# Row maxima of the attention scores from half-depth matmuls, two heads at once on the two halves of the array's rows, with the first pair issued one step earlier

## What is computed

```python
def one_block(qblk):
    s = jnp.einsum("bqkgd,bskd->bkgqs", qblk.astype(jnp.float32), kf) * scale
    p = jax.nn.softmax(s, axis=-1)
    return jnp.einsum("bkgqs,bskd->bqkgd", p, vf)
```

## Time and profile before

| what | value |
|---|---|
| median of 3 executions | 2594.71 us |
| lowest, highest | 2590.71, 2596.11 us |
| the profiled execution | 2592.71 us |
| span from its first to its last instruction | 2590.9 us |
| TensorE busy in the span | 96% |
| VectorE, ScalarE, GpSimd busy | 65%, 46%, 43% |
| mean granted TensorE clock | 0.99 of full |
| steps of phase2 (key heads 0 to 3) | about 929 to 1670 us |

### The profile page before, as it was taken

How to read it: one execution, slowest core, us unless ns; L and a number is a source line. 1 busy time by engine, 2 the same in 40 slices (tenths; PEclk the granted TensorE clock), 3 DMA queues, 4 the chain that set the end, 5 groups by cost and what they waited for, 6 DMA issues and landing times. The chain is left out here.

```text
span 2590.9 us, 40706 instructions
## 1 busy us (share of the span) xinstructions
PE 2477.0 (96%) x14413; PEld 2243.1 (87%) x14413; DVE 1692.4 (65%) x2527; ACT 1194.2 (46%) x2187; POOL 1101.8 (43%) x936
## 2 busy tenths in 40 slices
PE   5999999999999899999999989999899999999998
PEld 2899999999999887778878867799899999988886
DVE  5047456556558458787787767626977777776775
ACT  5223323323324246766666667645544444443442
POOL 1123132222223353433343233733667777756554
PEclk9999999999999999999999999999999999999999
DMA  9611111111111110010020010242122222245654
GB/s 328 207 35 45 36 52 44 37 43 44 37 43 30 50 34 9 11 54 9 9 65 9 1 55 27 91 119 74 48 72 76 76 76 76 76 159 204 222 199 142
DMA packets 193130, 195.66 MB, mean 76 GB/s; under 512 B 23516, under 2 KB 155772, under 8 KB 193020
## 3 DMA queue, kind: packets, MB, share of 16 engines
q1 hardware_dynamic: 191804, 189.52, 23.0%
q10 hardware_dynamic: 1216, 4.72, 0.5%
HBM read 162.22 MB, written 31.99 MB: 75 GB/s over the span
## 5 line engine op out<-in xcount | busy, mean ns | idle before, releaser
L395 PE MATMUL proj_ps<-act_hi,w_hi 128*128 128x384 f32 x1152 | 406.6, 353 | 3.3 <-ACTq L748 3.3
L397 PE MATMUL proj_ps<-act_hi,w_lo 128*128 128x384 f32 x1152 | 387.1, 336 | 0.0
L396 PE MATMUL proj_ps<-act_lo,w_hi 128*128 128x384 f32 x1152 | 386.9, 336 | 0.0
L571 POOL CAST w_hi<-w_raw 128x1024 fp32r<-128x1024 f32 x48 | 79.2, 1650 | 563.9 <-PE proj_ps L397 523.9
L1960 DVE TENSOR_TENSOR probs_lo<-mix_ps,probs_hi 128x512 fp32r<-128x512 f32 x324 | 222.9, 689 | 138.8 <-ACT mix_ps L1758 135.1
L2921 DVE SCALAR_TENSOR_TENSOR conv<-up,conv_t,conv 128x127 f32<-128x127 f32 (+4 forms) x264 | 242.1, 945 | 59.1 <-ACT conv L2701 53.5
L1757 ACT ACTIVATE probs_hi<-mix_ps 128x512 fp32r<-128x512 f32 x324 | 193.5, 597 | 174.8 <-PE mix_ps L1546 173.5
L395 PEld LDWEIGHTS proj_ps<-act_hi,w_hi 128*128 128x128 f32 x1152 | 217.6, 189 | 11.3 <-issue 4.3
L396 PEld LDWEIGHTS proj_ps<-act_lo,w_hi 128*128 128x128 f32 x1152 | 217.5, 189 | 2.8
L397 PEld LDWEIGHTS proj_ps<-act_hi,w_lo 128*128 128x128 f32 x1152 | 217.0, 188 | 0.0
L2969 DVE TENSOR_TENSOR sums_hi<-gated_raw,sums_hi 128x384 fp32r<-128x384 f32 x66 | 145.1, 2201 | 81.8 <-ACT sums_hi L2778 81.7
(11 more groups left out here) (341 smaller groups left out, 6895.7 us busy)
## 6 DMA issues: line engine op xcount, KB each, us to landing
w_raw<-in_w_down SPq DMA_DIRECT2D x66, 512.0 KB, 3.3
w_raw<-in_w_in SPq DMA_DIRECT2D x64, 512.0 KB, 3.8
w_raw<-in_w_up SPq DMA_DIRECT2D x44, 512.0 KB, 4.3
ada_w<-in_ada_w SPq DMA_DIRECT2D x7, 2048.0 KB, 15.8
gated_raw<-gated_scratch SPq DMA_DIRECT2D x66, 192.0 KB, 3.5
q_k_dec<-in_ada_w SPq DMA_DIRECT2D x5, 2048.0 KB, 7.9
gated_scratch<-gated SPq DMA_DIRECT2D x22, 288.5 KB, 2.1
gated_scratch<-gated SPq DMA_DIRECT2D x22, 287.5 KB, 2.1
```

What stands on the lines that cost most here:

```text
L395: nc.tensor.matmul(out, w_hi, x_hi, start=(k == 0), stop=False)
L396: nc.tensor.matmul(out, w_hi, x_lo, start=False, stop=False)
L397: return nc.tensor.matmul(out, w_lo, x_hi, start=False, stop=last)
```

## The change

The maxima are made from the high parts of the queries alone, over 64 rows of the array. The staging order of the queries is changed so that after the transpose heads 0 and 1 have their high parts on partitions 0 to 63, and heads 2 and 3 on partitions 64 to 127. `max_pair(s, j)` takes the place of `max_piece`: it waits until both banks are free and issues one matmul for a head of 0 and 1 on the lower 64 rows into `B_S` and one for the head two further on the upper 64 rows into `B_X`. The ten pieces keep their sizes; `PIECES` is reordered so that pieces 2j and 2j + 1 are pair j. Pair 0 of step s + 2 is issued at i = 9 of step s, behind `weighted`; pairs 1 to 4 of step s + 1 at i = 0 (behind `weighted`), 2, 4 and 6. For this `q_part(s + 2)` moves to i = 8, and `q_out(s + 2)` to i = 9 ahead of `exps(s + 1, 1)`. VectorE reduces the two pieces of pair 0 behind `low(s + 1, 1)`, and the others around `low`. In `context_step` the five pairs are issued with two fill units behind each from pair 2 on (key heads 0 and 3) or from pair 0 on (1 and 2), and pair 0 of the step after next at its end.

```diff
--- before.py
+++ after.py
@@ -1016,7 +1016,9 @@
         PL = sb("probs_lo", [P, 4, 512], F32R)
         QT1 = sb("q_t_hilo", [P, 2, 512], F32R)
         QT2 = sb("q_t_max", [HEAD + 1, 2, 512], F32R)
-        QS1 = sb("q_stage", [P, GQ, P], F32R)
+        QS1 = sb("q_stage", [P, 10 * HEAD], F32R)
+        Q_HI = QS1[:, :].rearrange("p (a c d) -> p a c d", a=2, d=HEAD)[:, :, 0:3:2, :]
+        Q_LO = QS1[:, HEAD:7 * HEAD].rearrange("p (a c d) -> p a c d", a=2, d=HEAD)[:, :, 0:3:2, :]
         QS2 = sb("q_stage_max", [P, GQ, HEAD + 2], F32R)
         ATT = sb("attn_t", [P, 2, T])
         ZA = sb("za_gate", [P, 2, T])
@@ -1114,9 +1116,9 @@
 
         S_USES = [(("k", 0, g), B_S) for g in range(4)] + [(("c", 0), B_S)]
 
-        PIECES = [(0, 0), (0, 1), (1, 0), (1, 1), (0, 2), (2, 0), (2, 1), (3, 0), (3, 1), (2, 2)]
+        PIECES = [(0, 0), (2, 0), (0, 1), (2, 1), (1, 0), (3, 0), (1, 1), (3, 1), (0, 2), (2, 2)]
         NP = len(PIECES)
-        PIECES_AT = [(0, 1), (2,), (3, 4), (5,), (6, 7), (8,), (9,), (), (), ()]
+        PAIR_AT = {0: 1, 2: 2, 4: 3, 6: 4}
         for s in range(NSTEP):
             kv, n = step_of(s)
             if n == 0 and kv + 1 < NKV:
@@ -1309,10 +1311,10 @@
                     if s:
                         pool.wait_ge(x_done, X_AT["q", s - 1] + 1)
                     pool.wait_ge(rope_ok, s + 1)
-                    q = QKV[:, n, 0:4 * HEAD].rearrange("p (h d) -> p h d", d=HEAD)
-                    nc.gpsimd.tensor_copy(QS1[:, :, 0:HEAD], q).then_inc(qs1_ok, 1)
+                    q = QKV[:, n, 0:4 * HEAD].rearrange("p (a b d) -> p a b d", a=2, d=HEAD)
+                    nc.gpsimd.tensor_copy(Q_HI, q).then_inc(qs1_ok, 1)
                     pool.wait_ge(qs1_ok, 2 * s + 1)
-                    nc.gpsimd.tensor_tensor(QS1[:, :, HEAD:P], q, QS1[:, :, 0:HEAD].bitcast(F32), ALU.subtract).then_inc(qs1_ok, 1)
+                    nc.gpsimd.tensor_tensor(Q_LO, q, Q_HI.bitcast(F32), ALU.subtract).then_inc(qs1_ok, 1)
 
                 def stage_q2(s):
                     kv, n = step_of(s)
@@ -1497,7 +1499,7 @@
                     pe.wait_ge(qs1_ok, 2 * s + 2)
                     pe.wait_ge(x_out, X_AT["q", s])
                     for h in range(GQ):
-                        m = nc.tensor.transpose(X[:, h * P:(h + 1) * P], QS1[:, h, :].bitcast(F32), ident[:, :])
+                        m = nc.tensor.transpose(X[:, h * P:(h + 1) * P], QS1[:, h * P:(h + 1) * P].bitcast(F32), ident[:, :])
                     m.then_inc(x_done, 1)
 
                 def q_max_part(s):
@@ -1517,20 +1519,28 @@
                         m = nc.tensor.matmul(bank[:, h * P:(h + 1) * P], QT1[:, s % 2, h * P:(h + 1) * P], KH[:, 0:P], start=True, stop=True)
                     m.then_inc(s_done, 1)
 
-                def max_piece(s, p):
-                    if p == 0:
+                def max_pair(s, j):
+                    if j == 0:
                         pe.wait_ge(x_out, X_AT["q", s] + 1)
                         pe.wait_ge(kh_out, 4 * (s // NS) + 4)
-                    pe.wait_ge(s_out, S_FREE["p", s, p])
-                    h, part = PIECES[p]
-                    bank = ps[:, (B_S, B_X)[p % 2], :]
-                    q = lambda h: QT1[:, s % 2, h * P:(h + 1) * P]
+                    pe.wait_ge(s_out, S_FREE["p", s, 2 * j])
+                    pe.wait_ge(s_out, S_FREE["p", s, 2 * j + 1])
+                    h, part = PIECES[2 * j]
+                    low, high = ps[:, B_S, :], ps[:, B_X, :]
+                    q_low = lambda h: QT1[0:HEAD, s % 2, h * P:(h + 1) * P]
+                    q_high = lambda h: QT1[HEAD:P, s % 2, (h + 2) * P:(h + 3) * P]
                     if part == 2:
+                        past = slice(9 * P, 11 * P)
                         for i in range(2):
-                            m = nc.tensor.matmul(bank[:, i * 2 * P:(i + 1) * 2 * P], q(h + i), KH[:, 9 * P:11 * P], start=True, stop=True)
+                            cols = slice(i * 2 * P, (i + 1) * 2 * P)
+                            m_low = nc.tensor.matmul(low[:, cols], q_low(h + i), KH[0:HEAD, past], start=True, stop=True)
+                            m_high = nc.tensor.matmul(high[:, cols], q_high(h + i), KH[HEAD:P, past], start=True, stop=True)
                     else:
-                        m = nc.tensor.matmul(bank, q(h), KH[:, P + part * 512:P + (part + 1) * 512], start=True, stop=True)
-                    m.then_inc(s_done, 1)
+                        keyed = slice(P + part * 512, P + (part + 1) * 512)
+                        m_low = nc.tensor.matmul(low, q_low(h), KH[0:HEAD, keyed], start=True, stop=True)
+                        m_high = nc.tensor.matmul(high, q_high(h), KH[HEAD:P, keyed], start=True, stop=True)
+                    m_low.then_inc(s_done, 1)
+                    m_high.then_inc(s_done, 1)
 
                 def scores_t(s, i):
                     x = chunk(s, i)
@@ -1584,7 +1594,7 @@
 
 
 
-                FILL_FROM = {0: 4, NKV - 1: 3}
+                FILL_FROM = {0: 2, NKV - 1: 2}
 
                 def context_step(s):
                     kv = s // NS
@@ -1599,11 +1609,11 @@
                                 gate_part(kv, t, k, k + 1)
                         del units[:count]
 
-                    for p in range(NP):
-                        max_piece(s + 1, p)
-                        if p >= FILL_FROM.get(kv, 0):
-                            fill(1)
-                        if p == 7:
+                    for j in range(NP // 2):
+                        max_pair(s + 1, j)
+                        if j >= FILL_FROM.get(kv, 0):
+                            fill(2)
+                        if j == 3:
                             weighted(s, 0)
                     fill(2)
                     q_max_part(s + 1)
@@ -1614,6 +1624,7 @@
                     fill(1)
                     q_part(s + 2)
                     fill(len(units))
+                    max_pair(s + 2, 0)
 
                 def step(s):
                     kv, n = step_of(s)
@@ -1625,15 +1636,17 @@
                         if n < 8:
                             if i == 9:
                                 scores_t(s + 1, 1)
-
-                            ahead = 1 if i else 0
-                            for p in PIECES_AT[i][:ahead]:
-                                max_piece(s + 1, p)
+                            if i and i in PAIR_AT:
+                                max_pair(s + 1, PAIR_AT[i])
                             weighted(s, i)
+                            if i == 0:
+                                max_pair(s + 1, PAIR_AT[0])
                             if i == 8:
                                 scores_t(s + 1, 0)
-                            for p in PIECES_AT[i][ahead:]:
-                                max_piece(s + 1, p)
+                                if s + 2 < NSTEP:
+                                    q_part(s + 2)
+                            if i == 9 and n < 7:
+                                max_pair(s + 2, 0)
                             if t is not None and i < 4:
                                 tile_part(kv, t, *TILE_AT[i])
                             if len(gates) == 2 and i < 4:
@@ -1654,7 +1667,7 @@
                                 q_max_part(s + 1)
                             if more and i == 8:
                                 scores_t(s + 1, 0)
-                    if s + 2 < NSTEP:
+                    if n == 8 and s + 2 < NSTEP:
                         q_part(s + 2)
 
                 for s in range(NSTEP):
@@ -1839,6 +1852,8 @@
                             gate_out(kv, gates[-1])
                         if n < 8 and i == 8:
                             q_max_out(s + 1)
+                        if n < 8 and i == 9 and s + 2 < NSTEP:
+                            q_out(s + 2)
                         if n == 8 and more:
                             if i == 1:
                                 keys_out(kv + 1, 0)
@@ -2024,15 +2039,18 @@
                     if go:
                         tile_gain(kv + 1, 0)
                     low(s + 1, 1)
+                    for p in range(2):
+                        row_max(s + 2, p)
 
                 def step(s):
                     kv, n = step_of(s)
                     t = tile_of(s)
                     more = kv + 1 < NKV
                     for i in range(10):
-                        if n < 8:
-                            for p in PIECES_AT[i][:1]:
-                                row_max(s + 1, p)
+                        if n < 8 and i in PAIR_AT:
+                            row_max(s + 1, 2 * PAIR_AT[i])
+                            if i == 6:
+                                row_max(s + 1, 2 * PAIR_AT[i] + 1)
                         if n == 8 and more:
                             if i == 1:
                                 tile_rope(kv + 1, 8)
@@ -2049,9 +2067,11 @@
                             low(s + 1, i - 8)
                         elif more and i == 8:
                             low(s + 1, 0)
```

(8 more changed lines are left out.)

## The result

The changed kernel takes 2650.22 us (median of four runs, 2648.28 to 2654.98), beside 2593.47 for the kernel before on the same chip: a ratio of 1.0221, interval 1.0208 to 1.0233, so 2.2% or 57 us slower. The forecast was slower by 18 us (2613), with a range up to 2645. The sign came as forecast; the time lies 5 us above the range. The mean granted TensorE clock of the profiled execution was 0.985, before 0.99.

The account below looks back on a forecast made before the run. TensorE, or its order with the loop through ScalarE and VectorE, was taken to set the pace. Border waits less pair savings, plus smaller terms, gave 17.4, say +18 us: 2613 us, range 2585 to 2645.

Parts of the forecast that it names:

- the wait ahead of pair 1: At a step border TensorE waits 1.4 us for both reductions of pair 0; the border ends 1.7 us later.
- I take nothing: Going between full array and row halves was costed at nothing; 0.21 us was kept only for the range.
- the half pair's 0.35: Pair on cached keys, four short matmuls with four weight loads: taken as 0.35 us, between 0.23 and 0.47.
- The 0.24: Cost in us taken for a pair of 512 columns on two row halves, near full overlap (0.23).
- eight pieces (1.84) become three pairs: After a step's first two pairs, 1.84 us becomes 0.83: 1.0 us saved per step, n = 1 to 7.
- its own rival of 2635: Rival: the halves don't overlap, so the 1.0 us saving is gone in 22 steps; 2635 us, chance 0.10.
- The rival of 29 us: Rival: borders of the halves cost 0.21 us per pair, 28 steps of five pairs; 2642 us, chance 0.12.
- key head 3, n = 2 to 7: Three borders with a gate's eviction at net +1.0 us each, three without filler at +0.2 each.
- from the product of a context step to the end of n = 1, four times: Pair 0 follows `q_part` directly with nothing between: +0.6 us each, +2.4 in all.
- idle time taken over from the old kernel: Some of the old 18.7 us TensorE idle ahead of the maxima is absorbed by new waits: -3 us.
- Faster: Rival: the wait ahead of pair 1 at i = 0 is small or absorbed by slack; 2573 us, chance 0.16.
- even: Rival: the border chain is 0.7 us shorter through partial overlap; 2595 us, chance 0.09.

Follow-up runs that it names:

- e6: Changed kernel with pair 1 issued a chunk later (i = 1, not i = 0) and every matmul 128 deep: 2621.7 us, 1.0106 of the kernel before.
- e1: Changed kernel with its order kept but each matmul of a pair 128 deep, so no halves: 2641.1 us, 1.0186 of the kernel before.
- e3: Changed kernel with both matmuls of a pair on the lower 64 rows, so they can't overlap: 2689.9 us, 1.0386 of the kernel before.
- e12: Changed kernel with every pair of 512 columns issued twice in a row: 2669.5 us, 1.0292 of the kernel before.
- e7: Kernel before, old order, with the pieces 65 rows deep: 2602.7 us, 1.0037 of the kernel before.
- e2: Kernel before, old order, with each piece one matmul on the lower 64 rows: 2695.4 us, 1.0395 of the kernel before.
- e5: Changed kernel, halves kept, with pair 1 issued a chunk later (i = 1, not i = 0): 2634.3 us, 1.0155 of the kernel before.
- e10: Changed kernel with nothing moved (pairs at i = 0, 1, 3, 4 and 6) and matmuls 128 deep: 2636.1 us, 1.0159 of the kernel before.
- e8: e6 with each matmul of a pair waiting for its own bank only: 2612.5 us, 1.0076 of the kernel before.

## Why the prediction was right or wrong

**The bound and the wait were right.** TensorE and the order on it set the pace; the wait ahead of pair 1 was forecast as 1.4 us and is 1.3, in the place and for the releaser that were named. e6 against e1 shows by removal that it costs: 19 us. It stands in 24 steps and not in some 28; its idle time is 26.7 us together, where about 35 stood.

**The step that failed is "I take nothing" for the borders of the halves**, with the half pair's 0.35. The body of a pair was right: 0.24, as e3 and e12 show. (The 0.24 was argued from column strips; that the row halves overlap as fully was a guess that came true.) But each pair pays 0.38 for going from the full array to the halves and back, and costs 0.62 or 0.63. For a step of key head 1 the account closes:

| term, us per step | forecast | measured |
|---|---|---|
| border, with pairs 0 and 1 in place of pieces 0 and 1 | +1.7 | 6.74 - 4.84 = +1.9 |
| eight pieces (1.84) become three pairs | 0.83 - 1.84 = -1.0 | 0.62 + 0.62 + 0.63 - 1.84 = 0.0 |
| the step | +0.7 | 25.40 - 23.40 = +2.0 |

The saving of 1.0 in a step became none. How much of the miss that is, the runs say. Without any saving the forecast is its own rival of 2635, 40 us over before; e1, which has no halves, is 49 over. The halves were to take 22 us off and put 8 on. So of the 39 us between the forecast's 18 and the measured 57, 30 belong to the halves and 9 to the order.

At full depth, e1, the same two terms are 6.82 - 4.84 = 2.0 and 3 x 0.47 - 1.84 = -0.4, together 1.6, and its step is 1.6 longer. That is also why halves and full depth differ by only 0.4 in a step: three pairs at 0.15, while pairs 0 and 1 stand ahead of a wait that absorbs their price.

**I had weighed the wrong pair of rows.** The earlier trace rows showed 0.21 for going in and out, L1560 in the earlier trace rows showed nothing, and I took the second because its data type and width were the same. But L1560 uses half of the columns and all rows. A pair uses half of the rows, and the price hangs on that: 65 rows pay nothing (e7), 64 rows pay 0.38 (e2). The Trainium skill ("TensorEngine Tiling (Array Packing)", Key Properties) has the rule that a change of tiling mode drains TensorE. The rows on the 64-row pairs agree with it: 0.09 us more ahead of a pair, and 0.42 instead of 0.23 behind it; a drain as such no row shows. The rival of 29 us, which I had given 0.12, had the right kind of cost and a price from the wrong row, 0.21 instead of 0.38. With 0.38, 28 steps of five pairs are 53 us on top of the forecast, 16 too much, because pair 1 and pair 0 of a step stand at a wait that absorbs their price (the border takes 6.74 us with halves and 6.82 at full depth).

**The other 9 us are terms of the order that were too small.** The profiled executions, cut where the last product of a step starts, give the whole of it (us more than before; the changed kernel's profiled execution was its slowest, 5 us above its median):

| stretch | forecast | after | e1 |
|---|---|---|---|
| key heads 1 and 2, n = 2 to 7 | +8.4 | +20.6 | +15.4 |
| key head 0, n = 2 to 7 | +6.0 | +9.9 | +8.2 |
| key head 3, n = 2 to 7 | +3.6 | +13.1 | +7.8 |
| from the product of a context step to the end of n = 1, four times | +2.4 | +9.4 | +7.4 |
| n = 8, and the context steps up to their product | 0 | +8.1 | +7.6 |
| idle time taken over from the old kernel | -3 | in the rows above | in the rows above |
| outside the attention | 0 | +1.2 | -0.2 |
| together | +17.4 | +62.3 | +46.2 |

The forecast's first three rows hold the saving of the halves, which e1 was not to have. Behind a context step TensorE stands idle 1.4 to 1.8 us ahead of pair 0 for the queries' copy, where +0.6 stood. The context steps were costed at 0 and are not free. Each late step of key head 3 grew by 1.0, where +0.2 stood, and e1 has 0.9 of that without halves: VectorE and the loop have less slack there than I gave them. All waits ahead of the pairs came to 54 us.

**The clock** took a part that no step of the forecast had. In key head 3, from the product of its context step to the last one of its step n = 7, the granted clock was 0.95 where the kernel before had 0.99 and e1 had 1.00, as the windows of that stretch show, for before, after, e1, e5 and e12:

```profile
1511.05:1656.44 145.39, 136.07 (x632) 104.41 (x630) 107.05 (x176) 101.07 (x189) 66.06 (x57) 0.99 0.21 68
```

```profile
1557.93:1719.79 161.86, 145.72 (x635) 102.41 (x634) 107.08 (x175) 102.22 (x189) 66.22 (x57) 0.95 0.19 61
```

```profile
1548.90:1704.12 155.22, 137.40 (x636) 103.50 (x634) 107.11 (x175) 102.04 (x189) 66.70 (x57) 1.00 0.20 63
```

```profile
1541.84:1709.37 167.53, 151.57 (x636) 104.99 (x635) 107.74 (x175) 102.22 (x189) 69.32 (x59) 0.90 0.18 59
```

```profile
1574.37:1735.37 161.00, 146.47 (x691) 100.76 (x690) 107.34 (x175) 102.19 (x189) 66.79 (x57) 0.99 0.19 61
```

Between after and e1 this stretch differs by 6.6 us, of the 16 between their two spans (the medians differ by 9). So a part of what the halves seem to cost there may be the lower of the two clock levels, 1.2 GHz, and not the passages (from 1568.90 to 1569.75 in the changed kernel matmuls of 512 columns start 0.43 us apart, where 0.23 is usual). I can't tell why it was granted: e5 with the same halves had 0.90, e12 with more of them 0.99, and each is one profiled execution. It stays open.

**The rivals.** No overlap (2635) is out: e3 shows that the overlap is real. Faster and even are out, since both asked for a shorter chain at the border. Of the marks that I had set for being wrong, two did not come (pieces' waits under 20 us; steps of key head 1 under 23.4), and the third did: the matmul behind a pair starts 0.42 us after it. That the sign came as forecast is owed to the order, which by e1 costs 49 us of the 57.

## What to carry to other kernels

In this kernel, packing two half-depth matmuls side by side saves one matmul's time, and pays once for each passage between the full array and its halves. Here the passage (0.38) cost more than one matmul of 512 columns (0.23), so by these numbers a packed group must hold at least two such pairs before it saves anything (0.86 for two, where four full pieces cost 0.93; not run as a kernel that saves). Count passages, not matmuls. For such a price look for a row with a matmul of the same shape: of the two rows at hand one had column strips and 0.21, the other half of the columns and nothing, and neither had the 0.38 of half of the rows.

Two units that fill two banks by turns hide the reduction of one behind the filling of the other. A change that fills both at once turns that into a wait of two reductions. Here pairing cost 43 us of 2593 at the same matmuls (e10, with the new places of the pairs), and of that kind of wait 9 us could be taken back by letting each matmul wait for its own bank (e8).

## What was new about the hardware

- A matmul of 64 rows between matmuls of the full array costs 0.38 us more than one of 65 rows or 128: 0.09 ahead of it, 0.11 after the matmul that follows, the rest at the pair itself. Two pairs in a row pay it once (0.62 for one pair, 0.86 for two).
- The two halves start 3 ns apart (the median of the pairs) and overlap in full, also with fp32r operands.
- A matmul on 64 of the 128 columns and all rows has the plain 0.23 behind it (L1560, and 1175.84 to 1176.07 above), while the column strips of the earlier trace rows paid 0.21 for going in and out. What sets these two apart was not tested.
